# The place of VectorE's low halves in a piece's work: from the beginning to the end

## What is computed

```python
# first block
u = rmsnorm(h, g_mix)
q, k, v, z, xbc, dt_raw, g_a, g_s = jnp.split(u @ w_in, offsets, axis=-1)
out_a = sliding_window_sink_attention(rope(q), rope(k), v) @ w_attn_br
xbc = silu(causal_depthwise_conv(xbc, conv_w, conv_b))
out_s = rmsnorm(ssd_chunked(xbc, dt, ...) * silu(z), g_ssd) @ w_ssd_br
h = h + (sigmoid(g_a) * out_a + sigmoid(g_s) * out_s) @ w_o
f = rmsnorm(h, g_ffn)
h = h + (silu(f @ w_gate) * (f @ w_up)) @ w_down
h = h + sigmoid(rmsnorm(h, g_ple) @ w_ple_gate) * (p @ w_ple_proj)
# second block
proj = rms_norm(x) @ w_in_2                      # q, kv, gate_logits, conv_in
attn = nsa_attention(q, kv, gates, ...)
conv = conformer_conv(conv_in, conv_w_2, ...)     # 31 taps, then a layer norm
x = x + jnp.concatenate([attn, conv], axis=-1) @ w_out_2
x = x + conv_glu_ffn(rms_norm(x), w_up_2, ffn_conv_w_2, ffn_conv_b_2, w_down_2)
out = rms_norm(x)
```

## Time and profile before

| | us |
|---|---|
| median of 3 runs | 2742.9 (2740.9 to 2743.19) |
| span of the profiled execution | 2741.4 |
| PE busy | 2706.7 (99%) |
| VectorE busy | 1961.1 (72%) |
| ScalarE busy | 1411.7 (51%) |
| low halves (888) on VectorE | 1039.4 |
| high halves (888) on ScalarE | 893.8 |

### The profile page before, as it was taken

One profiled execution on the slowest core, in us unless ns is written; L12 is line 12 of the kernel. 1 busy time (PEld: TensorE's weight loads), 2 busy tenths in 40 slices (PEclk: granted clock), 3 DMA queues, 4 the chain that ended last, 5 costly groups with the idle time before them and its releaser, 6 DMA issues.

```text
span 2741.4 us, 41654 instructions
## 1 busy us (share of the span) xinstructions
PE 2706.7 (99%) x16606; PEld 2376.5 (87%) x16606; DVE 1961.1 (72%) x2946; ACT 1411.7 (51%) x2092; POOL 105.6 (4%) x197
## 2 busy tenths in 40 slices
PE   8999999999999999999999999999999999999998
PEld 7878888888888888888888889998888888888887
DVE  7558778757677776677766678877787775677765
ACT  6455556544455554455545552247665553455543
POOL 1320000000000000000000000000000000000000
PEclk9999999999999999999999999999999999999999
DMA  7557556555568888888856556873455556555554
GB/s 241 153 179 226 175 184 200 185 184 186 200 218 288 286 283 288 294 283 283 284 200 211 179 175 228 311 264 121 140 190 185 190 197 190 182 193 185 185 195 143
DMA packets 168915, 581.58 MB, mean 212 GB/s; under 512 B 20129, under 2 KB 26993, under 8 KB 168209
## 3 DMA queue, kind: packets, MB, share of 16 engines
q1 hardware_dynamic: 152368, 526.06, 58.3%
q0 software_dynamic: 16208, 52.85, 5.2%
q10 hardware_dynamic: 144, 0.01, 0.0%
HBM read 535.06 MB, written 43.09 MB: 211 GB/s over the span
## 4 chain that ended last, share of the span: by engine, by line
PE 92%; DVE 4%; ACT 2%; DMA 1%; issue 1%; SPq 0%; POOL 0%; DVEq 0%; ACTq 0%; POOLq 0%
PE PS L956 91%; DVE wl L1921 1%; DMA raw<-in_w_in 1%; ACT wh L1379 1%; PE PS L1294 0%; ACT SX1b L1379 0%; DVE SQA L1921 0%; DVE H L1921 0%; ACT SX1a L1379 0%; DVE TA L1929 0%; DVE SX1b L2067 0%; DVE Z L1921 0%; DMA raw<-in_w_down 0%; DVE CC L1929 0%; ACT TB L1379 0%
## 5 line engine op out<-in xcount | busy, mean ns | idle before, releaser
L1921 DVE TENSOR_TENSOR wl<-raw,wh 128x1024 fp32r<-128x1024 f32 (+3 forms) x888 | 1039.4, 1195 | 464.2 <-ACT wh L1379 462.6
L1379 ACT ACTIVATE wh<-raw 128x1024 fp32r<-128x1024 f32 (+3 forms) x888 | 893.8, 1030 | 502.4 <-PE PS L956 401.4
L956 PE MATMUL PS<-CHt,wh 128*128 128x512 f32 x2816 | 885.9, 395 | 0.0
L956 PE MATMUL PS<-BIGt,wh 128*128 128x512 f32 (+1 forms) x2816 | 755.0, 356 | 1.5 <-issue 0.6
L956 PE MATMUL PS<-AHt,wh 128*128 128x512 f32 (+1 forms) x2080 | 636.5, 386 | 17.0 <-DVE wl L1921 16.9
L956 PEld LDWEIGHTS PS<-CHt,wl 128*128 128x128 f32 x2816 | 529.0, 188 | 124.8
L956 PE MATMUL PS<-CHt,wl 128*128 128x256 f32 x2816 | 553.5, 278 | 0.0
L956 PEld LDWEIGHTS PS<-BIGt,wl 128*128 128x128 f32 x2304 | 434.9, 189 | 79.0 <-issue 0.2
L956 PE MATMUL PS<-BIGt,wl 128*128 128x256 f32 x2304 | 497.8, 279 | 0.0
L956 PEld LDWEIGHTS PS<-BIGt,wh 128*128 128x128 f32 x2816 | 434.1, 190 | 6.3 <-issue 3.8
L956 PEld LDWEIGHTS PS<-AHt,wl 128*128 128x128 f32 x1952 | 368.5, 189 | 80.2 <-issue 0.7
(11 more groups left out here) (311 smaller groups left out, 1633.7 us busy)
## 6 DMA issues: line engine op xcount, KB each, us to landing
raw<-in_w_up SPq DMA_DIRECT2D x264, 512.0 KB, 4.9
raw<-in_w_in SPq DMA_DIRECT2D x196, 512.0 KB, 4.3
raw<-in_w_down SPq DMA_DIRECT2D x132, 512.0 KB, 4.3
raw<-in_w_gate SPq DMA_DIRECT2D x88, 512.0 KB, 5.4
raw<-in_w_down SPq DMA_DIRECT2D x56, 384.0 KB, 3.6
PKR<-in_w_in SPq DMA_DIRECT2D x36, 512.0 KB, 5.4
parked_halves<-PKH POOLq DMA_DIRECT2D x36, 512.0 KB, 5.9
parked_halves<-PKL POOLq DMA_DIRECT2D x36, 512.0 KB, 7.1
```

Source lines behind the costliest of these rows:

```text
L956: return e.matmul(o, l, r, start=start, stop=stop, skip_group_check=True)
L1379: return e.activation(o, x, f, **k)
L1921: return e.tensor_tensor(o, x, y, op)
```

## The change

VectorE gets a step of its own in the plan, `low`, and no longer works on `split`. In the first four pieces it stands right behind `split`, as before. In the loop the plan gathers the pieces split in this iteration in `lows` and lists their `low` behind evictions, convolution step and side step of the iteration. ScalarE's `split`, SP's `fetch`, the buffers and all waits are as they were.

```diff
@@ make_plan, the first four pieces
         plan.append(("seed", s, 0))
         plan.append(("split", s, 0))
+        plan.append(("low", s, 0))
         ns += 1
...
-    held, going, later = [], [], []
+    held, going, later, lows = [], [], [], []
@@ make_plan, iteration s
         while ns < len(subs) and ns <= s + lead(ns):
             if ns not in full and ns not in parked:
                 plan.append(("split", ns, 0))
+                lows.append(ns)
             ns += 1
...
             conv.step()
         if (s + 1) % u.pace == 0:
             side_step()
+        while lows:
+            plan.append(("low", lows.pop(0), 0))
         for x in [x for x in later if x[0] <= s]:
@@ VectorE
-        def split(s, _):
+        def low_part(s, _):
             cut, j = (slice(None), slice(0, words(s))), ring_no[s]
             e.wait_ge(split_hi.sem, split_no[s] + 1)
             tt(WL[j % NHL][cut], RAW[s % NRAW][cut], f32(WH[j % NHL][cut]), SUB).then_inc(split_lo.sem)
...
-        todo = dict(split=split, park=park, seed=seed, norm=norm, ...
+        todo = dict(low=low_part, park=park, seed=seed, norm=norm, ...
```

More of the change, by code:

```diff
@@ L2685, in evac @@
                 ends_of_units[u.ev](n, u)
-        todo = dict(split=split, park=park, seed=seed, norm=norm, sum_x=sum_x, rotary=rotary, rope_q=rope_q,
+        todo = dict(low=low_part, park=park, seed=seed, norm=norm, sum_x=sum_x, rotary=rotary, rope_q=rope_q,
                     rope_k=rope_k, attn1=attn1, cums=cums, conv4=conv4, ssd=ssd, load_p=load_p, join=join,
```

## The result

The changed kernel takes 2764.6 us (median of 4 runs, 2763.7 to 2765.1) against 2743.05 for before (the three runs of the table above and a fourth, 2740.9 to 2745.9): a ratio of 1.0076, 95% interval 1.0065 to 1.0088. It is 21.5 us slower. The forecast was 2770, with 2763 to 2777 as the likeliest case's own range: right in its direction, 5 us too high.

The account below looks back on a forecast made before the run. PE, busy 2706.7 of 2741.4 us, was taken as the bound, so only its waits matter. FFN2's +30.5 and -2.9 from the rest gave +27.6, 2769.0; with 1.5 for the runs' median 2770.5, rounded to 2770, range 2746 to 2786.

Parts of the forecast that it names:

- FFN2: Both FFN2 halves: a loop through fetch, high half, eviction and low half outlasts PE's unit; 1.49 us a pair, +30.5 us.
- The landing: FFN2 fetch started by the fourth low half: taken as 3.5 us; at the median of 5.0 the term would be +90.
- The estimate of 3.2 us: FFN2 landing for 512 KB by the skill's formula for GpSimd transfers; would give some 18 us and 2758.
- xbc: 95 to 210 us: queued work fills VectorE's idle time and the chain moves forward; -4.7 us, bounds 0 to 6.2.
- q: Around 55 us: one low half goes behind a rotation waiting for a DMA, PE later by a piece; +2.7 us.
- rival 4: PE's clock: each FFN2 stall brings on a half-clock stretch, +32 more, 2802; chance 0.05.
- The ple gate: 1580 to 1640 us: VectorE and ScalarE's round goes under 11.14 us, PE's waits go; -1.3 us.
- the wait for GCM: Between 1500 and 1700 us: PE's wait goes if the compression's work passes the low half; -1.8 us.
- The second attention: Attn2, with the rest of the kernel: no effect expected, 0.
- The two low halves: One in the long convolution, one in the pp units, behind work with little lead: +2.2 us together, bounds 0 to 5.6.
- The faster one: FFN2's loop does not close, high half does not delay the eviction or transfers land sooner; 2738, chance 0.10.
- The milder and heavier rounds: FFN2 landings of 2.9 to 3.3, 2754 (0.15); or landings of 3.8 to 4.0 or FFN1 stalls, 2784 (0.15).

Follow-up runs that it names:

- the kernel with FFN2 alone: Against the kernel before, low halves go behind the evictions only in iterations of g2 and u2, elsewhere the old order; 2769.6 us, ratio 1.0092.
- the kernel with the spare buffer: The whole change plus a fifth raw buffer in FFN2 for every second fourth piece; 2737.9 us, ratio 0.9980 against before.
- the kernel with one low half moved: Against the kernel before, only the low half of piece 39, in xbc, takes the new place; 2741.2 us, ratio 0.9994.
- the kernel with chosen stages: Against before, new place only in xbc, ple gate to compression and second attention (iterations 24-59, 536-603, 616-663); 2729.9 us, ratio 0.9954.

## Why the prediction came out right, and where it was off

**FFN2, +30.5 forecast, +25.7 measured.** The mechanism is shown: the round opened by a buffer takes the stall away, and 0.52 us put on the round costs 0.52 a unit. The size was off in two factors. A pair of units stalls 1.28 to 1.33 us (from piece 687 to 759 a pair takes 23.57 us, from 815 to 887 23.63; before 22.29), not 1.49. The links, read off the trace, are together some 0.09 us a unit shorter than in my sum: the eviction up to the low half 5.78 and 6.43 where I had 5.88 and 6.53 (steps that overlap by a few hundredths were added up whole), the landing 3.46 for 3.5, the low half 1.22 for 1.16. And 19.5 pairs are in the regime, not 20.5: the first half begins with four units without a stall, the second with three. The landing, the term with the widest bounds (+90 at a landing of 5.0), was 3.4 to 3.6 us each time, as the first of a burst had been in the earlier trace rows. The median over FFN2's fetches, which include those queued behind others, says nothing on a fetch that the round waits for. The estimate of 3.2 us worked out from the Trainium skill's page "DMA: Bandwidth & Descriptors" (section "Anatomy of one DMA — SWDGE (gpsimd) path") is about 0.3 us short here, in a round where 0.1 us costs 4 us in all.

**xbc, -4.7 forecast, -8.3 measured.** The waits of PE for low halves went from 6.2 to 0.6 us, 5.6 of it. A wait of 0.6 us for SX1b, in the attention beside it, is gone too. So are the 3.4 us at half speed after the long wait, with a piece of 4.42 us in the earlier trace rows. I had seen that row and priced it only as a rival that adds time, not as a gain when the wait in front of it goes. What it is worth is read from the kernel with FFN2 alone, which has the waits and not the stretch: it is 0.9 us ahead of before at piece 60, less than the 1.6 that the one piece is longer. The remaining 1.2 us are not traced.

**q, +2.7 forecast, +4.9 measured.** The chain of waits after the change, 50 to 66 us, and the stretches around 58.8:

```profile
50.84 4.96 DMA RO<-QT
...
57.84 1.15 DVE wl L1925
...
59.03 7.06 PE PS L960 x31
```

```profile
56.00:58.80 2.80, 0.00 (x0) 0.00 (x0) 2.77 (x4) 1.06 (x1) 0.42 (x1) 1.00 0.02 7
58.80:62.20 3.40, 3.17 (x10) 2.69 (x11) 3.37 (x6) 0.00 (x0) 1.54 (x4) 0.50 0.72 211
```

The mechanism is the one named: the low half stands behind a rotation that waits 4.96 us for a DMA. The rotation's DMA landed 0.7 us later than in the earlier trace rows, and PE, idle until 59.03, then ran 3.4 us at a granted clock of 0.50, the 1.2 GHz level: piece 15 took 4.51 us in place of 2.95. 2.7 + 0.7 + 1.6 is 5.0. The half clock belongs to the moved low half: all six traces with this order in q have it; why the DMA landed later is open, and these traces stand at 3.8 to 5.3 at piece 16. So rival 4's mechanism did occur, behind a wait of 4.1 us, and in FFN2 never, with stalls of up to 1.1 us a unit and a granted clock of 1.00.

**Small terms.** The ple gate gained 2.3 us (-1.3 forecast) and the wait for GCM went as said, a step of -1.8 at piece 582, with 0.4 lost again at piece 603. The second attention, put at 0 without a reason, gained 1.1 in each of the six traces with the moved order there; how was not traced. The two low halves of which I wrote "an estimate of +2.2 for both" cost +1.3 and +2.9 in the table, an uncertain 4.9 by the medians. In the pp units 0.7 of the 1.3 is in all five traces of kernels with the order moved there; the rest is scatter, which kernels with the order of before show as well (-0.4 to +0.7). VectorE in the long convolution:

```profile
1766.86 1.23 DVE L1925 TENSOR_TENSOR wl<-raw,wh 128x1024 fp32r<-128x1024 f32 x1
1767.99 2.47 DVE L1933 SCALAR_TENSOR_TENSOR CC<-Z,CV,CC 128x256 f32<-128x256 f32 x6
1770.37 1.23 DVE L1925 TENSOR_TENSOR wl<-raw,wh 128x1024 fp32r<-128x1024 f32 x1
1771.51 0.70 DVE L1925 TENSOR_TENSOR TC<-PS,RB 128x512 f32<-128x512 f32 x1
1772.11 2.47 DVE L1933 SCALAR_TENSOR_TENSOR CC<-Z,CV,CC 128x256 f32<-128x256 f32 x6
1774.48 1.24 DVE L1925 TENSOR_TENSOR wl<-raw,wh 128x1024 fp32r<-128x1024 f32 x1
```

VectorE has no idle time here and gives a low half every 3.5 us or more (1766.86, 1770.37, 1774.48), PE takes a piece in 2.9. Not one but four moved low halves (pieces 612 to 615) have each a convolution step of 2.4 us in front of them, and the last an eviction's 0.6 as well. Before, the first of them was ready 2.8 us ahead of PE and each later one 0.6 us less; I had counted only the last.

**Luck in the total.** Outside FFN2 the forecast was -2.9 and the trace shows -3.8, but not term by term: q is 2.2 worse than forecast and the two small low halves 2.0, xbc is 3.6 better and the other stages 1.4. That these misses nearly cancel is luck; FFN2's term is the one that carries the forecast.

**Rivals.** The faster one (2738) needed the round not to bite; it is what the kernel with the spare buffer does, 2737.9. The milder and heavier rounds fall with the landing of 3.5 us, and FFN1 has no wait of PE for a low half, though the longest landings there were 7.8 us.

## What to carry to other kernels

- When a step is moved later on one engine, write down what it releases and follow that until it comes back to the same engine: here the release of a buffer, a load, a conversion that stands before the work just passed. Compare that round with the period of the engine that sets the pace, not only the step's slack against its reader: the slack of 0.3 us was enough once the round was open, and worthless while it was closed.
- One more buffer on that round, for every second of the pieces that needed it, opened it without a change to the order (2764.6 to 2737.9 us). A place in the order that is right in one stage (xbc, with an idle VectorE and ready work behind) can be wrong in another (FFN2, the convolution): choosing by stage gave 2729.9 us, where all or nothing gave 2764.6 and 2743.
- Price a chain's landing by a load in the same position of its burst, not by the median of all.

## What the runs showed of the hardware

A wait of PE of a few us can cost more than itself. In q 4.1 us of waiting were followed by 3.4 us at a granted clock of 0.50, the 1.2 GHz level, which made one piece 1.6 us longer; all six traces with the moved low half there have such a stretch, none of the six others has. A shorter wait is not always followed by one. At piece 41, after a wait of 2.4 or 2.5 us, three traces with the order of before have it and one, that of FFN2 alone, has not; there it cost 0.9 us.

And a stretch at half clock can cost nothing. In the second attention six of the twelve traces have one, that of before and that of the change among them. First before, then the kernel with one low half moved, whose order there is that of before and which is 2.4 us ahead: the same 11.4 us of work, with PE's wait for ScalarE's PT2a in it:

```profile
1862.00:1873.40 11.40, 9.72 (x80) 8.61 (x81) 8.40 (x23) 11.15 (x31) 0.00 (x0) 0.85 0.30 93
...
PE PS L956 <- ACT PT2a L1379: 2.0, 2, 1.7
```

```profile
1859.60:1871.00 11.40, 8.35 (x80) 7.45 (x81) 8.39 (x22) 11.18 (x31) 0.00 (x0) 1.00 0.31 93
...
PE PS L963 <- ACT PT2a L1386: 3.3, 2, 1.7
```

Before ran 3.4 us of it at half clock (0.85 in the mean) and PE was busy for 9.72 us, at full clock for 8.35. But ScalarE is busy nearly all the time in both (11.15 and 11.18), and what the full clock gave PE, 1.4 us, it waited longer for ScalarE: from piece 612 to 636 the two traces take the same time. In the same way the change, with 3.4 us at half clock from 1861 us, and the kernel with chosen stages, with none, both gain 1.1 us there. So the 1.1 us are the order's, and of the 12.9 us that the trace of the best kernel gains only the stretch at 146 us, 0.9 us, has to do with the clock. What decides whether the clock falls was not tried.
